# Delta queries kept feature-major without norm, the residual's identity added on VectorE, and one score matmul over all key blocks

## The reference, cut to what matters

```
qkv = silu(depthwise_conv(x @ W_qkv))            # 8 heads of 128 for q, k, v
q = l2_normalize(q) * 128 ** -0.5 ; k = l2_normalize(k)
# gated delta rule in chunks, forward and backward; per chunk:
t_inv = inverse of (strict(beta * k k^T * decay) + I)     # "triangular solve"
qk = (q k^T) * decay
v_new = t_inv(v ...) - ... @ state ; o = (q * exp(g)) @ state + qk @ v_new
state = state * exp(g_last) + (k * ...)^T @ v_new
o = (o_fwd + o_bwd) ; o = o * rsqrt(mean(o * o) + 1e-6) * w * silu(z)
# windowed attention, 16 query heads on 4 key heads of width 64, blocks of 128 queries:
s = q_block @ [k_prev, k_own, k_next]^T * 64 ** -0.5, masked to |i - j| <= 128
p = softmax([s, sink])[:-1] ; o_sw = p @ v
```

## Time and profile before

| | us |
|---|---|
| median of three runs | 2354.21 |
| lowest and highest | 2350.39, 2355.19 |
| the profiled execution | 2352.94 |
| its span, from the first instruction to the last | 2351.1 |
| PE busy in it | 2268.6 (96%) |
| DVE busy | 1126.1 (48%) |
| POOL busy | 1145.8 (49%) |
| ACT busy | 841.9 (36%) |

### The profile page before, as it was taken

How to read it: one execution, slowest core, us unless ns; L and a number is a source line. 1 busy time by engine, 2 the same in 40 slices (tenths; PEclk the granted TensorE clock), 3 DMA queues, 4 the chain that set the end, 5 groups by cost and what they waited for, 6 DMA issues and landing times.

```text
span 2351.1 us, 34310 instructions
## 1 busy us (share of the span) xinstructions
PE 2268.6 (96%) x13528; PEld 1828.8 (78%) x13528; DVE 1126.1 (48%) x1960; ACT 841.9 (36%) x2252; POOL 1145.8 (49%) x674
## 2 busy tenths in 40 slices
PE   8999999989999999999999999999899998999997
PEld 6787888877777788888777778778677787888885
DVE  4677677764444611110257776777544476111003
ACT  3554445465541211110145554454665403111100
POOL 5453333324337466666545432333343385666664
PEclk9999999999999999999999999999999999999999
DMA  4221112111123232332232211211111332323322
GB/s 151 72 81 46 50 55 60 42 50 46 55 89 135 72 97 91 99 99 90 92 108 72 72 46 42 64 50 42 50 47 53 109 116 90 98 91 98 117 90 81
DMA packets 53887, 182.65 MB, mean 78 GB/s; under 512 B 7520, under 2 KB 8160, under 8 KB 53728
## 3 DMA queue, kind: packets, MB, share of 16 engines
q1 hardware_dynamic: 48976, 167.01, 22.1%
q10 hardware_dynamic: 4752, 13.45, 1.6%
HBM read 169.94 MB, written 4.19 MB: 74 GB/s over the span
## 4 chain that ended last, share of the span: by engine, by line
PE 88%; DVE 8%; issue 2%; ACT 1%; DMA 1%; POOL 0%; DVEq 0%; ACTq 0%; POOLq 0%
PE PS L583 19%; PE PS L585 18%; PE PS L584 18%; PE PS L751 12%; PE PS L843 2%; PE PS L957 2%; PE PS L1024 2%; PE PS L829 2%; PE PS L847 2%; PE PS L971 1%; PE PS L902 1%; PE PS L886 1%; PE PS L780 1%; PE PS L893 1%; PE PS L923 1%
## 5 line engine op out<-in xcount | busy, mean ns | idle before, releaser
L544 POOL TENSOR_SCALAR wh<-w_raw 128x1024 fp32r<-128x1024 f32 (+1 forms) x255 | 278.1, 1091 | 1034.3 <-DMA w_raw<-stream 1033.4
L547 POOL TENSOR_TENSOR wl<-w_raw,wh 128x1024 fp32r<-128x1024 f32 (+1 forms) x255 | 615.0, 2412 | 21.3
L583 PE MATMUL PS<-xh,wh 128*128 128x512 f32 x992 | 398.8, 402 | 8.6 <-issue 4.2
L585 PE MATMUL PS<-xl,wh 128*128 128x512 f32 x992 | 390.2, 393 | 0.0
L584 PE MATMUL PS<-xh,wl 128*128 128x512 f32 x992 | 389.6, 393 | 0.0
L583 PEld LDWEIGHTS PS<-xh,wh 128*128 128x128 f32 x992 | 188.1, 190 | 56.0 <-issue 10.8
L585 PEld LDWEIGHTS PS<-xl,wh 128*128 128x128 f32 x992 | 188.1, 190 | 40.8
L584 PEld LDWEIGHTS PS<-xh,wl 128*128 128x128 f32 x992 | 188.5, 190 | 37.1
L751 PE MATMUL PS<-xh,wh 128*128 128x512 f32 x448 | 206.2, 460 | 5.2 <-DVEq L1690 3.4
L1993 DVE TENSOR_TENSOR hf<-sg,PS 128x512 f32<-128x512 f32 x44 | 30.2, 687 | 359.9 <-PE PS L585 359.9
L1643 DVE SCALAR_TENSOR_TENSOR conv_acc<-PS,cw,conv_acc 128x510 f32<-128x510 f32 x192 | 143.9, 749 | 99.3 <-ACT conv_acc L1186 93.9
(11 more groups left out here) (287 smaller groups left out, 4828.0 us busy)
## 6 DMA issues: line engine op xcount, KB each, us to landing
w_raw<-stream SPq DMA_DIRECT2D x254, 512.0 KB, 3.4
w_raw_spare<-stream SPq DMA_DIRECT2D x46, 512.0 KB, 3.4
x<-x_in ACTq DMA_DIRECT2D x6, 512.0 KB, 7.8
qx<-qx SPq DMA_DIRECT2D x48, 64.0 KB, 2.0
raw<-raw SPq DMA_DIRECT2D x32, 64.0 KB, 2.0
ln_g<-ln_rows ACTq DMA_DIRECT2D x4, 512.0 KB, 4.2
ln_b<-ln_rows ACTq DMA_DIRECT2D x4, 512.0 KB, 5.2
x_park<-x ACTq DMA_DIRECT2D x4, 512.0 KB, 4.1
```

What stands on the lines that cost most here:

```text
L544: nc.gpsimd.tensor_scalar(wh[s][:, w], w_raw[s][:, w], 1.0, 1.0, ALU.mult, ALU.mult).then_inc(w_hi_done, 1)
L547: nc.gpsimd.tensor_tensor(wl[s][:, w], w_raw[s][:, w], wh[s][:, w].bitcast(F32), ALU.subtract).then_inc(split_done, 1)
L583: mm(o, ah, bh, start=first, stop=False)
L585: return mm(o, ah, bl, start=False, stop=last)
```

## The change

- **Delta queries.** The convolution's result for the eight query tiles is written straight into raw in feature-major form. It is still transposed for the sum of squares, but the transposed tile is no longer copied out, the queries are no longer multiplied by their reciprocal norm, and qn and qT and their second transpose are gone. The products that took qT take raw[:, h]. The norm is applied at the end instead: the square on ACT takes it as its scale, and rno is multiplied by it (one more DVE instruction of 128x28 and one of 128x4 per layer, each behind a wait).
- **The residual's identity.** id_16 becomes id_e, the identity times 1024. The identity product is gone; V is now made on DVE by one instruction: PSUM times 1024 plus id_e. On DVE the two instructions stand behind front_scale and ahead of the scaled keys.
- **Scores.** One product of 64x128 by 256 or 384 columns takes the place of two or three of 128 columns.
- Since raw[0..7] holds the queries until the end of the heads, z moves up by one tile: z of head 0 has a place of its own (z_first), z of head n is in raw[n-1]. The attention's result overwrites z in pairs, so the low parts of z are made as 3, 2, 2 and 1 tiles instead of four times 2, on ACT and POOL.

```diff
                 def front_turn(m, t):
-                    for b, src in ((4, qn), (5, kn[t])):
-                        pe.wait_ge(qk_normed, m * 2 + b - 3)
-                        for c in range(CHUNKS):
-                            ins = nc.tensor.transpose(PS[:, b, c * P:(c + 1) * P], src[:, c, :], ident)
-                        ins.then_inc(qk_turned, 1)
+                    pe.wait_ge(k_normed, m + 1)
+                    for c in range(CHUNKS):
+                        ins = nc.tensor.transpose(PS[:, 5, c * P:(c + 1) * P], kn[t][:, c, :], ident)
+                    ins.then_inc(k_turned, 1)
...
                     for r in range(2):
                         pe.wait_ge(y_upd[r], n * 7 + 7)
-                        mm(PS[:, 3 * r, :].rearrange("p (c t) -> p c t", c=CHUNKS), id_16[:], rows(id_16[:]), start=True,
-                           stop=False, skip_group_check=True)
                         for c in range(CHUNKS):
                             o = PS[:, 3 * r, c * P:(c + 1) * P]
-                            mm(o, NAh[r][:, c, :], Y[r][:, c, :], start=False, stop=False, skip_group_check=True)
-                            ins = mm(o, NAl[r][:, c, :], Y[r][:, c, :], start=False, stop=True,
-                                     skip_group_check=True)
+                            mm(o, NAh[r][:, c, :], Y[r][:, c, :], start=True, stop=False)
+                            ins = mm(o, NAl[r][:, c, :], Y[r][:, c, :], start=False, stop=True)
                         ins.then_inc(e_mm[r], 1)
...
                     for t in range(2):
-                        for j in range(hi - lo):
-                            for half in range(2):
-                                part = slice(half * HD, (half + 1) * HD)
-                                mm(PS[:, half * 2 + t, j * P:(j + 1) * P], qx[part, g * 2 + t, b * P:(b + 1) * P],
-                                   kz[part, g, (lo + j) * P:(lo + j + 1) * P], start=j == 0, stop=lo + j == b,
-                                   skip_group_check=True)
+                        for half in range(2):
+                            part = slice(half * HD, (half + 1) * HD)
+                            mm(PS[:, half * 2 + t, 0:(hi - lo) * P], qx[part, g * 2 + t, b * P:(b + 1) * P],
+                               kz[part, g, lo * P:hi * P], start=True, stop=False, skip_group_check=True)
...
                 def conv_activate(i, s):
                     act.wait_ge(conv_step, (l * U_QKV + i * 2 + s + 1) * (CONV - 1))
-                    A(conv_act[s][:], conv_acc[s][:], ACT.Silu).then_inc(conv_silu, 1)
+                    silu = flat(raw[:, i * 2 + s, :, :]) if i * 2 < HEADS else conv_act[s][:]
+                    A(silu, conv_acc[s][:], ACT.Silu).then_inc(conv_silu, 1)
...
                 def front_turned(m, t):
-                    for b, dst, done in ((4, qT[t], qT_ready), (5, kT[t], kT_ready)):
-                        act.wait_ge(qk_turned, m * 2 + b - 3)
-                        copy(dst[:].rearrange("p c t -> p (c t)"), PS[:, b, :]).then_inc(done, 1)
+                    act.wait_ge(k_turned, m + 1)
+                    copy(flat(kT[t][:]), PS[:, 5, :]).then_inc(kT_ready, 1)
...
-                    for r in range(2):
-                        act.wait_ge(e_mm[r], n + 1)
-                        A(V[r][:].rearrange("p c t -> p (c t)"), PS[:, 3 * r, :], ACT.Copy,
-                          scale=E_SCALE).then_inc(e_ready[r], 1)
...
                         ins = A(raw[:, bass.ds(h + 2 * HEADS, 1), c, :].rearrange("p a t -> p (a t)"),
                                 o_dn[:, bass.ds(h, 1), c, :].rearrange("p a t -> p (a t)"), ACT.Square,
+                                scale=rn[:, h, c:c + 1],
                                 accum_out=rno[:, bass.ds(h, 1), c].rearrange("p a -> p a"))
...
                 def front_scale(h, m, t):
-                    for u, dst in ((0, qn), (HEADS, kn[t])):
-                        src = raw[:, bass.ds(h + u, 1), :, :].rearrange("p a c t -> p (a c) t")
-                        TT(dst[:], src, cols(rn[:, bass.ds(h + u, 1), :].rearrange("p a c -> p (a c)")),
-                           ALU.mult).then_inc(qk_normed, 1)
+                    TT(kn[t][:], raw[:, h + HEADS, :, :], cols(rn[:, h + HEADS, :]), ALU.mult).then_inc(k_normed, 1)
...
                     if more:
                         front_scale(h + 1, n + 1, 1 - s)
+                    for r in range(2):
+                        dve.wait_ge(e_mm[r], n + 1)
+                        STT(V[r][:], bank(3 * r), E_SCALE, rows(id_e[:]), ALU.mult, ALU.add).then_inc(e_ready[r], 1)
                     fill_out(ISSUED[h, "L6"])
                     scaled_keys(n, s)
...
                 nc.vector.reciprocal(rno[:, HEADS - 1, :], rno[:, HEADS - 1, :]).then_inc(rno_dve, 1)
+                dve.wait_ge(rno_dve, l * 6 + 5)
+                TT(rno[:, HEADS - 1, :], rno[:, HEADS - 1, :], rn[:, HEADS - 1, :], ALU.mult).then_inc(rno_dve, 1)
```

More of the change, by code:

```diff
@@ L172, in trunk @@
         id_bf = place("id_bf", [P, P], BF16)
-        id_16 = place("id_16", [P, P], F16)
+        id_e = place("id_e", [P, P], F16)
         minus_id = place("minus_id", [P, P], F32)
@@ L218, in trunk @@
         blk = [P, CHUNKS, P]
-        qn = head_buf("qn", blk)
-        kn, qT, kT = ([head_buf(f"{name}{s}", blk) for s in range(2)] for name in ("kn", "qT", "kT"))
+        kn, kT = ([head_buf(f"{name}{s}", blk) for s in range(2)] for name in ("kn", "kT"))
         QKT = [[head_buf(f"QKT{s}{r}", blk) for r in range(2)] for s in range(2)]
@@ L249, in trunk @@
         bdl = [head_buf(f"bdl{r}", [P, CHUNKS]) for r in range(2)]
-        assert work[0] <= big + 112 * KB
+        assert work[0] <= big + 110 * KB
+        z_first = place("z_first", [P, SEQ], F32, big + 110 * KB)
         ozh = place("ozh", [P, KT, SEQ], F32R, big + 64 * KB)
@@ L291, in flat, with z_tile @@
             return ap.rearrange("p c t -> p (c t)")
+        def z_tile(n):
+            return z_first[:] if n == 0 else flat(raw[:, n - 1, :, :])
         def side_tiles(j):
@@ L358, in trunk @@
         head_cols = sem("head_cols")
-        qk_normed = sem("qk_normed")
-        qk_turned = sem("qk_turned")
-        qT_ready = sem("qT_ready")
+        k_normed = sem("k_normed")
+        k_turned = sem("k_turned")
         kT_ready = sem("kT_ready")
@@ L555, in _ @@
                     if 0 <= f < KT // 2:
-                        for i in (2 * f, 2 * f + 1):
+                        for i in range(2 * f + (f > 0), min(2 * f + 3, KT)):
                             pool.wait_ge(oz_hi, l * KT + i + 1)
-                            nc.gpsimd.tensor_tensor(ozl[:, i, :], flat(raw[:, i, :, :]), ozh[:, i, :].bitcast(F32),
+                            nc.gpsimd.tensor_tensor(ozl[:, i, :], z_tile(i), ozh[:, i, :].bitcast(F32),
                                                     ALU.subtract).then_inc(oz_lo, 1)
@@ L777, in front_products @@
                     pe.wait_ge(decay_done, m * 2 + b - 3)
-                    src, done = (kT[t], kk_done) if b == 4 else (qT[t], kq_done)
+                    src, done = (kT[t][:], kk_done) if b == 4 else (raw[:, m % HEADS, :, :], kq_done)
                     for c in range(CHUNKS):
@@ L922, in head @@
                                 pe.wait_ge(o_out[r], n * 4 + step)
-                                mm(PS[:, 2 + r, 0:P], qT[s][:, chunk[r], :], S[r][(step - 1) % 2][:], start=True,
+                                mm(PS[:, 2 + r, 0:P], raw[:, h, chunk[r], :], S[r][(step - 1) % 2][:], start=True,
                                    stop=True).then_inc(qs_mm[r], 1)
@@ L1123, in fill_out @@
                         if kind in "zg":
-                            nc.scalar.copy(flat(raw[:, n + (HEADS if kind == "g" else 0), :, :]),
+                            nc.scalar.copy(z_tile(n) if kind == "z" else flat(raw[:, n + HEADS, :, :]),
                                            src).then_inc(fill_free[p % 2], 1)
@@ L1198, in keep_tokens @@
                         for c in range(CHUNKS):
-                            A(sq[:, c, :], PS[:, 2 + s, c * P:(c + 1) * P], ACT.Square,
-                              accum_out=rn[:, bass.ds(i * 2 + s, 1), c].rearrange("p a -> p a"))
+                            ins = A(sq[:, c, :], PS[:, 2 + s, c * P:(c + 1) * P], ACT.Square,
+                                    accum_out=rn[:, bass.ds(i * 2 + s, 1), c].rearrange("p a -> p a"))
+                    if i * 2 < HEADS:
+                        ins.then_inc(tok_stored, 1)
+                        return
                     nc.scalar.copy(raw[:, bass.ds(i * 2 + s, 1), :, :].rearrange("p a c t -> p (a c t)"),
@@ L1362, in _ @@
                 fill_out(ORDER.index(("v", 0, FILL.index(("v", 0)))) + 1)
-                act.wait_ge(rno_dve, l * 4 + 4)
+                act.wait_ge(rno_dve, l * 6 + 6)
                 head_out(HEADS - 1)
@@ L1378, in _ @@
                     if n < KT // 2:
-                        for i in (2 * n, 2 * n + 1):
```

(9 more changed lines are left out.)

20 lines of the change are left out of this document (9 added, 11 removed).

## The result

| | before | after |
|---|---|---|
| median of seven runs each, us | 2353.67 | 2360.79 |
| lowest and highest | 2350.39, 2356.45 | 2359.13, 2362.21 |
| ratio, with its 95% interval | | 1.0035 [1.0025, 1.0044] |
| the profiled execution | 2352.94 | 2360.95 |
| its span | 2351.1 | 2359.0 |

What follows compares the result with a forecast made beforehand. PE, busy 96%, bounds the kernel, with DVE's chain close behind. Corrections +4.2, transposes -0.9, scores -2 and tail +0.4 make +1.7; with the clock's +3.4 on 2352.94 that gives 2358.0 us, range 2340 to 2366.

Steps and rivals of the forecast that it cites:

- Scores: Wider score products on PE in 32 groups: between 0 and 2.9 us less, taken as 2.
- PE alone: Rival: PE's work is all that counts, the first recurrence product follows PE in every head; 2337.4 us, chance 0.13.
- V on DVE: DVE's new V in each head: 0.6 us apart, bounds 0.35 and 2.4, and not held up by POOL.
- The rival with a slow V: V takes 2.4 us on DVE instead of 0.6, late for L871 in 8 heads; 2372 us, chance 0.02.
- kb behind POOL's low split: First and fifth heads: kb waits for POOL's L547, first recurrence product at 6.40 us, 1.56 later in each of four; +6.2.
- E0: Start of the residual in a head's correction, the zero from which the prediction counts times; 195.46 us in the first head before.
- The other heads: Corrections: four heads without POOL -1.8 us, second heads +1.1, sixth -1.0, seventh +0.6, last -0.9.
- Tail: Behind each layer's last head, rno's further small DVE instruction in a chain PE waits for: +0.2 us a layer, +0.4.
- The clock: Four PE waits of 2.4 us in the heads, one in two ending in a clock fall: +3.4 us, between 0 and 6.8.
- The rival in which the clock falls every time: Slower still: V holds back L902 by 1.56 us in four heads, each with a clock fall; 2361.4 us, chance 0.15.
- POOL, shifted against PE, also meets DVE's products: Part of the slower-still rival, at the next head's front: one more meeting a head of 0.3 us, 2366; chance 0.15.
- the idle time of the first recurrence product's line: Sign on PE: idle grows from nearly nothing to some 15 us; under 5 us the forecast fails, time below 2345.

## Why the prediction was right

**What bounds the kernel.** The step that mattered was the distance of 0.03 us by which YF was hidden in the earlier trace rows. Taking 0.87 us off PE there gave only 0.44 in the heads without POOL, and beside the split it gave nothing, since DVE's chain took over: in the fifth head of the changed kernel it is DVE alone from V to YF. Had PE alone counted, 2337.4 was the time, and the kernel with the keys behind YF, where that is nearly so, measured 2337.87. That these agree to half a microsecond is partly luck: its corrections gave 15.1 us and not 13, and it has waits for the keys (2.8) and for the masked V (1.4 more than before) that the sum of that rival doesn't have.

**V on DVE.** Estimated at 0.6 apart and 0.69 long, from the YF row; measured 0.685, with POOL's L547 beside it (in the first head 193.47 to 194.52) or not. The rival with a slow V falls.

**kb behind POOL's low split.** Place and size were as worked out. Start forecast at 1.85 behind E0, measured 194.77 - 192.91 = 1.86; end forecast 0.41 behind the split's end, measured 0.42; first and fifth heads forecast +6.2 together, measured +6.25 (25.60 less 19.35). In all four kb ends 0.41 to 0.42 behind the split. The memset takes the split's reading away and leaves the order, and with it kb's 2.64 fall to 0.55: shown, not only argued. The Trainium skill has a rule for this case (SBUF — State Buffer, "Who interferes with whom"): a DVE instruction with two SBUF inputs contends with a GpSimd one that reads SBUF, not with one that only writes it. The trace agrees on both halves, 2.64 us beside the split and 0.55 beside the memset.

**The other heads.** Third and fourth: forecast 4.41, measured 4.41 in all four. Second: forecast +1.1, measured +0.7; in layer 1 it is 5.43 as forecast (5.42), in layer 0 kb took 1.05 and the head only 0.08 more. Sixth: -1.0, measured -1.3. Seventh: +0.6, measured +0.4. Last: -0.9, measured -0.8. Together +4.2 forecast, +3.4 measured. All the small shifts of POOL against DVE were right in sign.

**The rest.** Transposes between projections: -0.9 as forecast. Scores: forecast -2, measured -1.2. It is the term that was mis-sized. From start to start a pair of 128 columns takes 0.112 us and one of 384 takes 0.322, so three narrow pairs in one save 0.013 us, 0.006 for each pair that goes and not 0.015. Narrow and wide groups of scores both lose 0.10 us at their first pair, and the group of L1024 that they were compared with the earlier trace rows only 0.05, so the doubt that the two rows differ in how they begin was right. Tail: forecast +0.2 a layer, +0.5 measured in layer 0 and not readable in layer 1. Of the sums of the prediction one doesn't quite close: its own terms give the chances 0.30, 0.28 and 0.42 for faster, same and slower, where it says 0.29, 0.27 and 0.44.

**The clock.** Forecast: four waits of 2.4 us, one in two ending in a fall, +3.4. Measured: waits of 2.17 to 2.35 us, with a fall behind two of the four (376.0 and 1372.7). The other two falls of the changed kernel stand behind waits for the masked V (352.1, 1529.7). Before had two as well, one behind a wait for the masked V (1522) and one behind a fill's wait for DVE (1389). One in two was a guess from two rows, and that it came out is luck; in the kernel with the residual's part alone it was three of four. The rival in which the clock falls every time gave 2361.4, close to the result, but its mechanism is not the one seen.

**What it left out of the sum.** POOL, shifted against PE, meets DVE's products of the next head's front, and they stand still. That was named in a rival only ("POOL, shifted against PE, also meets DVE's products") and is a part of the result: +2.0 us in the waits of L844. Between the third and the fourth head:

```profile
348.04 2.44 POOL L550 TENSOR_TENSOR wl<-w_raw,wh 128x1024 fp32r<-128x1024 f32 x1
...
348.76 2.00 DVE L1608 TENSOR_TENSOR X<-NAh,lev_mask 128x512 f16<-128x512 f16 x1
...
352.02 0.53 PE L844 MATMUL PS<-V,X 128*128 128x128 f16 x4 [1.85 <-DVE V L1726]
```

Before, that product took 0.66 us in layer 0, but 2.00 at the same place of layer 1. A fall of the clock stands right behind this wait too (352.1), and one 1.7 us behind the longest of its kind (1529.7). The new V on DVE isn't needed for it: these waits are 12.4 us without the residual's part, 12.1 with that part alone and 12.0 with the keys behind YF, against 10.6 before. A shift of the engines by any of these edits seems to be enough, but what sets it in each case stays open. With the low split as a memset they are 7.8.

Forecast were 5.1 us (1.7 and 3.4). The waits for the masked V add 2.0 and the missing part of the scores 0.8, the corrections take 0.8 off, and the tail adds 0.1, which makes 7.2. What is missing to the 7.9 of the span no term names.

**What would show it.** It was the idle time of the first recurrence product's line, forecast at some 15 us: 16.2. The other signs came as well: kb took 2.46 to 2.64 us in the four heads, and the group of four pairs of 384 columns 1.49 us.

## What to carry to other kernels

Taking work off the busiest engine is worth little where the next engine's chain is a few hundredths of a microsecond behind it: read that distance in the timeline first, and if work is added to the second chain, move whatever isn't needed yet behind what the first engine waits for. Here that was one line, and it turned +0.35% into -0.65%. Where two engines can block each other, keep instructions that can be blocked from standing ahead of one that is waited for. To dodge one meeting by shifting it, as with the keys ahead of V, here moved it to the next.

## What the runs showed of the hardware

- In the first head, a wait of 0.40 us of DVE for PE ahead of V, together with V itself, which doesn't hold POOL up, was enough for POOL's 2.39-us split to get in ahead of kb. Before, DVE's unbroken products held POOL's first instruction to 1.77 us; after, it took 1.05 and the second came 0.1 later.
- Which of two instructions gets through is not told by starts that lie close together: with POOL's record 0.13 us ahead of kb's, kb got through three times and was held once; at 0.16 us and more it was held in all four.
- Small and 16-bit instructions of DVE are held as long as wide ones: 0.17 became 1.67 for a copy of 40 columns, 0.41 became 2.00 for a 16-bit product with a mask.
- A pair of 64-row products of 384 columns takes 0.322 us from start to start, three pairs of 128 columns 0.335: the narrow ones lose 4%.
- Waits of PE of about the same length end in a fall of the clock or not, in the same kernel and the same place of different heads: two of four at 2.2 to 2.4 us, three of four at 2.0 to 2.1.
